# The output projection's matmuls of 512 moving columns become two of 256 each

## The reference

```python
merged = g[:, :, 0] * ua + g[:, :, 1] * ub + g[:, :, 2] * um
x = x + (merged @ w_out[l]).astype(x.dtype)
```

## Time and profile before

| | us |
|---|---|
| median of 3 runs | 1233.57 |
| lowest and highest | 1233.3, 1234.34 |
| span of the profiled execution, first to last instruction | 1231.0 |
| TensorE matmuls busy (5596 of them) | 1207.6 |
| TensorE weight loads busy (5596) | 1004.3 |
| VectorE busy | 681.2 |
| ScalarE busy | 535.0 |
| output projection, first matmul to last | 1139.1 to 1227.0 |

### The profile page before, as it was taken

How to read it: one execution, slowest core, us unless ns; L and a number is a source line. 1 busy time by engine, 2 the same in 40 slices (tenths; PEclk the granted TensorE clock), 3 DMA queues, 4 the chain that set the end, 5 groups by cost and what they waited for, 6 DMA issues and landing times.

```text
span 1231.0 us, 14994 instructions
## 1 busy us (share of the span) xinstructions
PE 1207.6 (98%) x5596; PEld 1004.3 (82%) x5596; DVE 681.2 (55%) x871; ACT 535.0 (43%) x672; POOL 35.1 (3%) x22
## 2 busy tenths in 40 slices
PE   8959999999999999999999999999999999999998
PEld 7847888888888888888888888888888888888887
DVE  6617555465565565556556556556555555555643
ACT  4615434444444444453454453434444443443432
POOL 0100000000000000000001000000000000000000
PEclk9989999999999999999999999999999999999999
DMA  9537654565555564554555565548548546755761
GB/s 324 207 125 245 224 181 160 173 206 171 172 197 171 177 207 160 194 198 161 181 186 176 174 199 169 200 148 258 185 158 252 186 167 208 226 203 178 275 215 51
DMA packets 121460, 235.40 MB, mean 191 GB/s; under 512 B 7576, under 2 KB 11853, under 8 KB 120909
## 3 DMA queue, kind: packets, MB, share of 16 engines
q1 hardware_dynamic: 108592, 218.44, 52.3%
q10 hardware_dynamic: 12828, 16.42, 4.6%
HBM read 231.16 MB, written 6.06 MB: 193 GB/s over the span
## 4 chain that ended last, share of the span: by engine, by line
PE 96%; ACTq 2%; DMA 1%; DVE 0%; ACT 0%; issue 0%; SPq 0%; DVEq 0%
PE acc L962 30%; PE acc L964 30%; PE acc L963 30%; ACTq L408 2%; PE side L985 2%; DMA w_raw<-in_x_dram 1%; PE side L1002 1%; PE side L1026 1%; PE side L998 1%; PE side L1016 1%; DMA w_raw<-in_w_in_dram 1%; PE side L1034 0%; PE side L1036 0%; PE side L1032 0%; PE side L1003 0%; PE side L1091 0%
## 5 line engine op out<-in xcount | busy, mean ns | idle before, releaser
L602 DVE TENSOR_TENSOR w_lo<-w_raw,w_hi 128x1024 fp32r<-128x1024 f32 x408 | 498.3, 1224 | 504.3 <-ACT w_hi L338 504.2
L338 ACT ACTIVATE w_hi<-w_raw 128x1024 fp32r<-128x1024 f32 x408 | 430.8, 1060 | 601.1 <-PE acc L964 587.5
L962 PE MATMUL acc<-w_hi,hT_hi 128*128 128x512 f32 x1152 | 454.0, 394 | 0.9 <-DVE hT_lo L624 0.5
L964 PE MATMUL acc<-w_hi,hT_lo 128*128 128x512 f32 x1152 | 449.0, 390 | 0.0
L963 PE MATMUL acc<-w_lo,hT_hi 128*128 128x512 f32 x1152 | 448.3, 389 | 0.0
L964 PEld LDWEIGHTS acc<-w_hi,hT_lo 128*128 128x128 f32 x1152 | 216.2, 188 | 45.8
L962 PEld LDWEIGHTS acc<-w_hi,hT_hi 128*128 128x128 f32 x1152 | 216.4, 188 | 45.0 <-DVE w_lo L602 0.8
L963 PEld LDWEIGHTS acc<-w_lo,hT_hi 128*128 128x128 f32 x1152 | 216.5, 188 | 43.3
L962 PE MATMUL acc<-w_hi,mT_hi 128*128 128x512 f32 x256 | 101.9, 398 | 15.1 <-DVE w_lo L602 15.1
L964 PE MATMUL acc<-w_hi,mT_lo 128*128 128x512 f32 x256 | 100.3, 392 | 0.0
L963 PE MATMUL acc<-w_lo,mT_hi 128*128 128x512 f32 x256 | 100.2, 391 | 0.0
(11 more groups left out here) (138 smaller groups left out, 550.4 us busy)
## 6 DMA issues: line engine op xcount, KB each, us to landing
w_raw<-in_w_in_dram SPq DMA_DIRECT2D x143, 1024.0 KB, 4.9
w_raw<-in_w_mem_kv_dram SPq DMA_DIRECT2D x16, 1024.0 KB, 5.1
w_raw<-in_w_out_dram SPq DMA_DIRECT2D x16, 1024.0 KB, 5.1
w_raw<-in_w_proj_a_dram SPq DMA_DIRECT2D x12, 1024.0 KB, 5.0
w_raw<-in_w_proj_m_dram SPq DMA_DIRECT2D x8, 1024.0 KB, 5.0
w_raw<-in_w_proj_b_dram SPq DMA_DIRECT2D x8, 1024.0 KB, 5.0
group<-bias_tiles ACTq DMA_DIRECT2D x5, 768.0 KB, 4.2
group<-in_b_gate_dram ACTq DMA_DIRECT2D x12, 256.0 KB, 5.9
```

The lines of the kernel that those rows point to most:

```text
L338: act.activation(whi[:, s % RING], raw[:, slot, UK * (s % 2):UK * (s % 2) + UK], ACT.Copy)\
L602: dve.tensor_tensor(wlo[:, s % RING], raw[:, (s // 2) % RING, UK * (s % 2):UK * (s % 2) + UK], whi[:, s % RING].bitcast(F32), ALU.subtract ...
L962: pe.matmul(banks[t][:], hi, whi[:, s % RING, j], start=first and j == 0, stop=False)
L964: return pe.matmul(banks[t][:], lo, whi[:, s % RING, j], start=False, stop=last and j == UK - 1)
```

## The change

Every matmul of the output projection is issued as two, over columns 0 to 255 and 256 to 511 of the same bank. The order inside a unit is: high by high for both halves, high by low for both, low by high for both, for each feature block and token block as before. The stationary operand is the same for the two halves. Only the first half's first matmul of a chunk carries the start flag, only the last half's last one the stop flag. Waits and semaphore updates stay at the same places, on the first and the last matmul of a unit. Lines further down move by 22.

```diff
+            def half_passes(s, k, j, t, bank, first, last):
+
+                tok = slice(t * P, (t + 1) * P)
+                hi, lo = mT[0][:, k + j, tok], mT[1][:, k + j, tok]
+                for c in (slice(0, CW // 2), slice(CW // 2, CW)):
+                    pe.matmul(bank[:, c], hi, whi[:, s % RING, j, c], start=first and j == 0 and c.start == 0,
+                              stop=False, skip_group_check=True)
+                for c in (slice(0, CW // 2), slice(CW // 2, CW)):
+                    pe.matmul(bank[:, c], hi, wlo[:, s % RING, j, c], start=False, stop=False, skip_group_check=True)
+                for c in (slice(0, CW // 2), slice(CW // 2, CW)):
+                    o = pe.matmul(bank[:, c], lo, whi[:, s % RING, j, c], start=False, stop=last and j == UK - 1 and c.start > 0,
+                                  skip_group_check=True)
+                return o
...
+            def out_unit(u0, s, k, banks, first, last):
+
+                pe.wait_ge(lo_done, u0 + s + 1)
+                for j in range(UK):
+                    for t in range(TT):
+                        o = half_passes(s, k, j, t, banks[t], first, last)
+                o.then_inc(unit_used, 1)
...
                 if s < NCH * CU - 1:
-                    unit(u0, s, mT, UK * (s % CU), acc[(s // CU) % 2], s % CU == 0, s % CU == CU - 1)
+                    out_unit(u0, s, UK * (s % CU), acc[(s // CU) % 2], s % CU == 0, s % CU == CU - 1)
                     continue
 
                 pe.wait_ge(lo_done, u0 + s + 1)
                 for t in range(TT):
                     for j in range(UK):
-                        o = passes(s, mT, UK * (s % CU), j, t, acc[(s // CU) % 2], False, True)
+                        o = half_passes(s, UK * (s % CU), j, t, acc[(s // CU) % 2][t], False, True)
                     o.then_inc(tail_done, 1)
```

## The result

The kernel takes 1237.95 us, median of 5 runs (1237.63 to 1239.1), against 1233.57. The ratio to the kernel before is 1.0038, with a 95% interval of 1.0025 to 1.005: slower, by more than the 0.2% that can be told from no change. The profiled execution took 1237.73 us with a span of 1236.0, which is 5.0 us more than the span before. The medians are 4.4 us apart; what lies around the span is 1.7 us here, and I had counted 2.57 before. In the executions of the kernel before that were run beside w504, the time is 1.7 to 1.9 us over the span. So the execution profiled before was itself some 0.8 us under its median, and the 2.57 us of the table and of the forecast are partly that: the medians' 4.4 us and the spans' 5.0 don't contradict each other.

A forecast was written before the change was run, and what follows sets the result against it. TensorE's matmul count times start interval was taken as the bound. Split and loads summed to 0.0 us on the 1231.0 us span; with the median 2.57 us above it, the forecast was 1233.6 us, range 1232.7 to 1237.4.

The forecast's parts named there:

- 2.57: Whole kernel: the median of the runs lies 2.57 us above the profiled span of 1231.0, giving 1233.6.
- What bounds the kernel: Whole kernel: time is the number of TensorE matmuls times their start interval; TensorE busy 1207.6 of 1231.0 us.
- The interval of 256 columns: Output projection: a half starts every 113.5 ns, as the forget gate's matmuls do; two take 227.0 against 226.8 ns.
- 0.1 us in the sum: Output projection: predicted cost of the split, 384 x (227.0 - 226.8) = +0.1 us, taken as nothing.
- The reading of the surplus: TensorE matmuls: 13.5 ns over 512 columns and 6.8 over 256 go with the columns, no price per matmul.
- The load under a half: Output projection: a full 128-column weight load fits beside a half's 113.5 ns, about 2 ns to spare; cost nothing.
- The longer of stream and load: Output projection: a half's interval is whichever is longer, column stream or weight load, taken as 113.5 ns.
- The one case at 57.38: Last forget gate matmul, 256 columns: a full load starts beside it and the next matmul follows 0.11 us on.
- Rival 1: Output projection: the weight load decides the interval, +2.7 to +3.8 us, 1236.3 to 1237.4; chance 0.13.
- Rival 2: Output projection: load doesn't run beside the stream (+84 us), or a half waits for its record (+60 us); chance 0.04.
- Rival 3: Output projection: sequencer falls behind at 120 ns a pair, +5.0 us, or instruction fetches stop TensorE, +2.7 us; chance 0.07.
- Rival 4: Output projection: a half is faster than the forget gate's, 108 ns, -4.2 us (1229.4); chance 0.05.

The follow-up runs named there:

- w504: Kernel before the change with output projection matmuls of 504 instead of 512 columns, last 8 of each bank left out; starts 226.7 ns apart.
- relock128: Changed kernel with a 128-column transpose ahead of the output projection's units, interrupting the row of halves; settles at 120.0 ns in all 31 rows.
- half_outer: Changed kernel with all three passes of the first half, then all three of the second; 120.0 ns a half, 1238.35 us, ratio 1.0034.
- same_dst: Changed kernel with both halves written to columns 0 to 255 of the bank, full loads; 120.0 ns a half.
- mov_tokens: Changed kernel with the forget gate's 256 transposed tokens as moving operand instead of half of the weights, full loads; 120.0 ns a half.
- w192: Kernel before the change with output projection matmuls of 192 instead of 512 columns, full loads; starts 111.7 ns apart as a mean.
- relock8: Changed kernel with 8 loaded columns and a transpose ahead of the units; of 31 rows, 25 settle at 116.7 ns and six at 120.0.
- gate_like: Changed kernel with 8 loaded columns, tokens as moving operand and always the same destination columns; settles at 120.0 ns, by way of 116.7 and 115.6.
- m64_again: Changed kernel with 64 instead of 128 loaded columns, half of the tokens left out, ten runs; median 1233.66 us, ratio 1.0001.
- m64_w256: Changed kernel with 64 instead of 128 loaded columns, first profile; 120.0 ns a half in the first four units, then 113.3 ns.

## Why the prediction was wrong

**What bounds the kernel** was right: the time moved by what the interval of TensorE moved, and by nothing else. ScalarE and VectorE stayed ahead, and the restarts and the end cost what they did, within 0.1 us.

**The interval of 256 columns** is the step that failed. I took 113.5 ns from the forget gate's row as the property of a matmul of that type and width. It isn't: the same form, with its 8 loaded columns, settles at 113.3, 115.6, 116.7 or 120.0 ns, and with a full load I saw an unbroken row settle at nothing but 120.0, in the changed kernel and in relock128, half_outer, same_dst and mov_tokens. 0.1 us in the sum should have been 768 x 120.0 - 384 x 226.7 = 5.1 us.

**The reading of the surplus** made it worse. 13.5 ns over 512 columns and 6.8 over 256 looked like a price for columns. With a full load it is the same 13.3 ns for 512, 400, 384, 320 and 256 columns, a price for each matmul, and the split doubles their number: 384 x 13.3 = 5.1 us. I had set aside the rule of the Trainium skill ("TensorE: Matmul & The Clock Gate", "Back-to-back issue gap") because the surplus was 13.5 and 6.8 ns, not 2.5 twice. The runs show that the form of that rule, a fixed sum on top of the columns, holds for the full load at five of the six widths (504 is 3.3 ns over it), and its size not: 13.3 ns here. Two points with different loads can't tell a fixed price from one that grows with the width.

**The load under a half.** That a full load fits beside a half was right, for a reason that was right: it needs 112 ns at most (w192). "The longer of stream and load" was wrong all the same, since 120.0 is longer than either. The one case at 57.38, 0.11 us with a full load beside 256 columns, was a single interval out of a row that had settled with other loads. In most runs here the first intervals after a change vary by several ns (116 to 121 in relock128), so one of them says nothing on where a row settles. The trace of before had a hint: the matmuls behind 57.49 start at 57.72, 57.96 and 58.19, up to 0.24 us apart, where they settle at 0.227.

**Rival 1** (the load decides) had the side and nearly the size, +2.7 to +3.8 us, and its marks in the profile nearly came true: starts 120.0 ns apart where it had 116 to 119, and load records of 192. Its mechanism, a load that takes longer than the stream, fell: rows with loads of 8 columns settle at 120.0 ns too, and a full load can follow every 111.7. Its marks weren't marks of its own. What is left of it is that no unbroken row of halves with a full load settled under 120.0 and some with smaller loads did, so a part of the load in the 120.0 isn't excluded. **Rival 2** fell: the loads run beside the stream, at 120.0 ns too. **Rival 3** had the number, 120 ns a pair and +5.0 us, by luck. Its mechanism fell: the same 768 pairs are issued every 113.3 ns with 64 loaded columns, and pairs in w192 every 111.7. In the changed kernel the interval is 120.0 ns from the first unit on and doesn't lengthen, and no longer gap stands beside the six packets of instructions in the stage. **Rival 4**: 113.3 ns is to be had with 64 loaded columns, but no row settled under it.

**The range** ended at 1237.4, 0.55 us short, because its upper end was rival 1's load on top of 113.5. The surplus that each matmul already had, taken as fixed, would have been the natural upper bound: 226.8 + 13.5 for a pair, +5.2 us.

**What stays open** is what picks the interval. It isn't the load's size alone or chance from run to run, nor, with a full load, the destination, the moving operand or the order of operands. Rows of the same instructions that begin differently settle differently (relock8). Why 64 columns settle at 113.3 ns in both profiles, why 8 in the forget gate do and in gate_like don't, where the 13.3 ns of a full load come from, and why 504 columns take as long as 512, no run here tells.

## What to carry to other kernels

Where TensorE is never idle, a matmul that is cut in two can cost something even if nothing of it shows as idle time. With the full stationary operand of 128 columns it was 13.3 ns each, 5.1 us for 384 cuts; with one of 64 columns the same cuts cost nothing once the row had settled at 113.3 ns, half of 226.7 (m64_again, 1.0001 of the kernel before). So with full loads use the widest moving operand that a bank takes, and expect nothing from cutting a little off it either: 504 columns took as long as 512. Take a price for an instruction from rows that have the same shape on both operands, and test a fixed price against one that grows with the size before the sum rests on it. A steady interval holds only for the row in which it was read: a small surplus in a long stream of matmuls is best bounded by the largest that any row of that kind shows.

## What was not expected of the hardware

A row of equal matmuls can settle at different intervals. 256 fp32r columns showed 113.3, 115.6, 116.7 and 120.0 ns, at a granted clock of 1.00, with the same instructions within one run (relock8: 116.7 in 25 rows, 120.0 in six), and the repeated runs of two programs gave the same time again. After most interruptions some five to ten intervals vary before they settle (five to eight in relock128); some rows are at 120.0 at once (m64_w256, six in relock8). A load of 128 columns repeats every 111.7 ns beside 192 fp32r columns, whose own 80.0 ns are the shorter part, so nothing shows that this width itself is slow.
